# Attention block B of a fused model kernel: projection items, weight fetches and head units in another order, and the compression in one PSUM bank

## Chip, cores and metric

The kernel is one program on one NeuronCore of a Trainium2 chip. The metric is device time in microseconds (us) of one execution, lower is better.

## What is computed

The input is a residual stream x of 256 tokens by 1024 features, all in float32. Four layers of "feed-forward, attention, feed-forward" follow each other; the attention kinds are A, B, C and A again. After them comes one further block, a hybrid of attention and a state-space part (H) with a mixture of experts. The change is about the attention of kind B, layer 1. It has three branches that share the queries; their gated outputs are added:

```python
q, kc, vc, ks, vs, kw, vw, gate = jnp.split(h @ w_in, splits, axis=-1)   # 1024 | 6 x 256 | 48 columns
kc_b = compress_kv(kc, cmp_pos[0], cmp_w1[0], cmp_w2[0])                 # gelu(blocks @ w1) @ w2, 15 blocks
vc_b = compress_kv(vc, cmp_pos[1], cmp_w1[1], cmp_w2[1])
s_cmp = einsum("bsgrd,bngd->bgrsn", q, kc_b) * scale                     # 16 heads x 256 queries x 15
o_cmp = einsum("bgrsn,bngd->bsgrd", masked_softmax(s_cmp), vc_b)
o_slc = selected_block_attention(q, ks, vs, sel_idx, rel_table)          # all 4 blocks chosen: plain causal
o_win = banded_attention(q, kw, vw, rel_table, B_WINDOW)                 # window 512 > 256: plain causal
o = g0 * o_cmp + g1 * o_slc + g2 * o_win
return o.reshape(B, S, -1) @ w_out
```

## The kernel before

Every engine has its own instruction list, written out by hand; semaphores order them. Within an engine the order is fixed: what waits holds up all that stands behind it.

**Weights.** SyncE (SP) streams all weights through a ring of three slots, one "fill" of up to 3 MB after the other, strictly in the order of the list `loads` (`stream_weights`). Fill n may be issued when the last user of fill n-3 is done, and each of its three parts (`sem_raw[0..2]`) when the same part of fill n-1 has landed. Block B has nine fills: `win` (0), the two halves of the query weights `qs[0]`, `qs[1]`, `slc`, `kvc` (the columns of kc and vc), the two first-layer weights of the compression (`b_cmp_w1`, `w1_fill` and the one after it, 2 MB each) and the two halves of `b_w_out`. Before, their order is win, qs[0], qs[1], slc, kvc, w1 of the keys, w1 of the values, w_out, w_out. TensorE waits for all three parts of a fill before its first product with it (`wait_fill`).

**Items.** The input projection is cut into 22 items of 16 matrix products each (`items`; form T gives features on partitions and is evacuated by VectorE, form N gives tokens on partitions and is evacuated by ScalarE). `project(q)` computes item q in a PSUM bank that alternates between 2 and 3. Items 0 to 8 (`ahead`) run before the attention; the others are handed out to the steps by `b["steps"]`. Items with `zc` are the columns that the compression reads, items with `both` are key tiles, each evacuated in four copies.

**Units and steps.** The attention is cut into 24 units: a quad of four heads, a half `a` of the queries (`a` = 0 has 128 keys, `a` = 1 has 256) and a branch `s` (1 window, 0 selected, here called local, 2 compressed, here called short). The first 16 units are scored, the eight short ones are not. Step j of every engine's list holds, in this order on TensorE: scores of unit j, transposes of the probabilities of unit j-2, the items of the step, a part of the compression (`pe_compress`, steps `cmp_step` to `cmp_step` + 4), from step `wo_step` = 22 on an eighth of the output projection (`output_first`), and the value products of unit j-2. VectorE does `coefficients(j-1)`, `biased(j)` (scale, bias, maximum), evacuations, `dve_compress`, `copy_out(j-2)`. ScalarE does `copy_pT(j-2)`, `exps(j)`, evacuations, `act_compress`. GpSimd scales the probabilities (L1715). So a scored unit runs around this loop: scores on TensorE, `biased` on VectorE, `exps` on ScalarE, `coefficients` on VectorE, scaling on GpSimd, transposes on TensorE, copy on ScalarE (L1692), values on TensorE, `copy_out` on VectorE.

Before, the order is the 8 window units, the 8 local units, the 8 short units. Items run in steps 0 to 9 (steps 6, 7 and 8 have two), the compression in steps 10 to 14 with `cmp_blocks` (L1773) made by VectorE in step 9. The two products with `w1` are L1836, the compressed scores are the 64 small products of L1865, and the softmax of the compressed branch is L1792 to L1808. Its probabilities must be there before the first short unit.

After the steps, the second half of the output projection (`output(1, ...)`, L1499) waits in A, B and C for `copy_out` of the last unit:

```python
    pe.wait_ge(K.sem.oT_sb, b["outs"])
    for a in range(NT):
        for half in range(2):
            output(1, a, half).then_inc(K.sem.y_done, 1)
```

Of the kernel before, what the change touches and what calls it, by code (L numbers as in the profile page):

```python
# [17 lines left out]
P = 128  # L18
# [227 lines left out]
class Program:  # L246
# [281 lines left out]
    def mixer_layout(self, b):  # L528
# [19 lines left out]
        if kind == "A":  # L548
# [8 lines left out]
            b["ahead"] = 6  # L557
            b["steps"] = [[6], [7], [8], [9], [10]]
            b["need_qk"] = [4, 6, 8, 10]
            b["need_v"] = [[2, 3]] * 4  # L560
            b["wo_step"] = 6
            wo = ins["a_w_out"][b["j"]]
        elif kind == "B":
            w = ins["b_w_in"][0]
            win = cols(w, (2048, 560))
            qs = [cols(w, (512 * c, 512)) for c in range(2)]
            slc = cols(w, (1536, 512))
            kvc = cols(w, (1024, 512))
            T(win, 0, None, both=4)
# [3 lines left out]
            T(win, 128, None, both=6)  # L573
            for r in range(1, 8):
                Q(qs[r // 4], r)
            T(slc, 0, None, both=0)
            T(slc, 128, None, both=2)
            N(slc, 256, 256, [self.v[:, a, 0:256] for a in range(NT)])
            for kv in range(2):
                for c in range(2):  # L580
                    T(kvc, 256 * kv + 128 * c, None, zc=(kv, c))
# [6 lines left out]
            b["w1_fill"] = len(loads)  # L588
            for kv in range(2):
                loads.append(("rows", ins["b_cmp_w1"][0, kv], 0, CMP_ROW_TILES))  # L590
            wo = ins["b_w_out"][0]
        elif kind == "C":
# [16 lines left out]
            Q(qs[1], 6), K(6), Q(qs[1], 7), K(7), V(1, 1)  # L609
            b["ahead"] = 7  # L610
            b["steps"] = [[7, 8], [9, 10], [11, 12], [13, 14], [15, 16], [17, 18], [19]]
            b["need_qk"] = [5, 9, 13, 18]
# [767 lines left out]
def units_of(b):  # L1380

    att, units, si = b["attn"], [], 0
    if b["kind"] == "H":
        order = [(a, quad, 0) for a in range(NT) for quad in att.quads]
    else:
        order = [(a, quad, s) for s in ((1, 0, 2) if b["kind"] == "B" else (0,)) for quad in att.quads for a in range(NT)]
    for u, (a, quad, s) in enumerate(order):
        scored = s < 2
        units.append(dict(a=a, quad=quad, s=s, si=si if scored else None, q=u, u=u, stage=u // 8, first=True, last=True,
                          nk=N_CMP if not scored else SEQ if b["kind"] == "H" else P * (a + 1)))  # L1390
        si += scored
    return units
# [5 lines left out]

def item_bank(q):

    return 0 if q == 0 else 2 if q % 2 else 3


def pe_mixer(K, pe, b):
# [12 lines left out]
    def product(q, k):  # L1417
        it, bank = items[q], item_bank(q)
# [113 lines left out]
    for j in range(len(units) + 2):  # L1532
        if j < len(units) and units[j]["si"] is not None:
            scores(units[j])
        if j >= 2:
            transposes(units[j - 2])
        for q in b["steps"][j] if j < len(b["steps"]) else ():
            project(q)
        if b["kind"] == "B":
            pe_compress(K, pe, b, j - b["cmp_step"])  # L1540
        if j >= b["wo_step"] and done < 4:
            output_first(done)
            done += 1
        if j >= 2:
            values(units[j - 2])
    while done < 4:
        output_first(done)
        done += 1
    pe.wait_ge(K.sem.oT_sb, b["outs"])
    for a in range(NT):  # L1550
        for half in range(2):
            output(1, a, half).then_inc(K.sem.y_done, 1)


def dve_mixer(K, dve, b):
# [4 lines left out]
    def evacuate_turned(q):  # L1560

        it, bank = items[q], item_bank(q)
        if it["form"] != "T":
# [63 lines left out]
    def copy_out(x):  # L1627
        dve.wait_ge(K.sem.oPV, U0 + x["u"] + 1)
        dst = K.oT[:, 2 * x["quad"]:2 * x["quad"] + 2, x["a"] * P:(x["a"] + 1) * P]
        src = K.psum[:, 6 + x["u"] % 2, 0:2 * P].rearrange("p (t s) -> p t s", t=2)  # L1630
        if x["stage"]:
            dve.wait_ge(K.sem.oT_sb, Q0 + x["u"] - 7)
# [11 lines left out]
    for j in range(len(units) + 2):  # L1644
        if 1 <= j <= len(units) and units[j - 1]["si"] is not None:
            coefficients(units[j - 1])
        if j < len(units) and units[j]["si"] is not None:
            biased(units[j])
        for q in b["steps"][j] if j < len(b["steps"]) else ():
            evacuate_turned(q)  # L1650
        if kind == "B":
            dve_compress(K, dve, b, j - b["cmp_step"])
        if j >= 2:
            copy_out(units[j - 2])


def act_mixer(K, act, b):
# [4 lines left out]
    def evacuate_tokens(q):  # L1662

        it = items[q]
        if it["form"] != "N":
            return
        act.wait_ge(K.sem.proj, b["item0"] + q + 1)
        r2 = K.st[:, PRE_R + it["a"]:PRE_R + it["a"] + 1]
        nc.scalar.activation(it["dst"], K.psum[:, item_bank(q), 0:it["n"]], ACT.Sigmoid if it.get("gate") else ACT.Copy,
                             scale=r2).then_inc(K.sem.evac_act, 1)  # L1670
# [26 lines left out]
    for j in range(len(units) + 2):  # L1697
        if j >= 2:
            copy_pT(units[j - 2])
        if j < len(units) and units[j]["si"] is not None:  # L1700
            exps(units[j])
        for q in b["steps"][j] if j < len(b["steps"]) else ():
# [53 lines left out]
def dve_compress(K, dve, b, step):  # L1756
# [8 lines left out]
    if step == -1:  # L1765
        dve.wait_ge(K.sem.cmp_small, 64)
        wait_evac(K, dve, b, len(b["items"]) - 1)
        for kv in range(2):
# [6 lines left out]
    if step == 2:  # L1775
        dve.wait_ge(K.sem.chidT_ps, 1)
        nc.vector.tensor_copy(K.chidT[:, :, :, :].rearrange("p v j n -> p (v j n)"),
                              K.psum[:, 2, 0:4 * G_B * N_CMP]).then_inc(K.sem.chidT, 1)
    if step == 3:
        dve.wait_ge(K.sem.kcb_ps, 1)  # L1780
        nc.vector.tensor_copy(K.kcb[:, :], K.psum[:, 3, 0:G_B * N_CMP])
        nc.vector.tensor_copy(K.vcb[0:N_CMP, :, :].rearrange("p g d -> p (g d)"), K.psum[0:N_CMP, 2, SEQ:SEQ + G_B * HD])\
            .then_inc(K.sem.kcb, 1)
# [27 lines left out]
def act_compress(K, act, b, step):  # L1811
    nc = K.nc
    if step == 1:
        act.wait_ge(K.sem.slots_used, K.fills[b["fill0"] + b["w1_fill"] + 1][1] + 1)
        nc.scalar.activation(K.chid[0:G_B * N_CMP, :, :],
                             K.psum[0:G_B * N_CMP, 2:4, 0:SEQ], ACT.Gelu_apprx_tanh).then_inc(K.sem.gelu, 1)
    if step == 4:
# [6 lines left out]
def pe_compress(K, pe, b, step):  # L1824
    nc, M = K.nc, G_B * N_CMP
    if step in (0, 1):
# [3 lines left out]
        for j in range(3):  # L1830
            pe.wait_ge(K.sem_raw[j], landed)
        wait_evac(K, pe, b, len(b["items"]) - 1)
        wait_evac(K, pe, b, len(b["items"]) - 2)
        w1 = K.raw[:, slot, 0:CMP_ROW_TILES * SEQ].rearrange("p (r f) -> p r f", f=SEQ)
        for r in range(CMP_ROW_TILES):
            ins = nc.tensor.matmul(K.psum[0:M, 2 + kv, 0:SEQ], K.z2[:, kv, r, :], w1[:, r, :],  # L1836
                                   start=r == 0, stop=r == CMP_ROW_TILES - 1)
        ins.then_inc(K.sem.slots_used, 1)
    if step == 2:
        pe.wait_ge(K.sem.gelu, 1)  # L1840
        for kv in range(2):
            for j in range(2):
                o = (2 * kv + j) * M
                ins = nc.tensor.transpose(K.psum[:, 2, o:o + M], K.chid[0:M, kv, j * P:(j + 1) * P],
                                          K.ident[0:M, 0:M])
        ins.then_inc(K.sem.chidT_ps, 1)
    if step == 3:
# [5 lines left out]
        for g in range(G_B):  # L1853
            for j in range(2):
                ins = nc.tensor.matmul(K.psum[0:N_CMP, 2, SEQ + g * HD:SEQ + (g + 1) * HD],
                                       K.chidT[:, 1, j, g * N_CMP:(g + 1) * N_CMP], K.cw2[:, 1, j, :],
                                       start=j == 0, stop=j == 1)
        ins.then_inc(K.sem.kcb_ps, 1)
    if step == 4:
        pe.wait_ge(K.sem.kcb, 1)  # L1860
        for a in range(NT):
            for h in range(NH):
# [43 lines left out]
def hybrid_bank(q):  # L1906

    return (0, 2, 3, 1, 5)[q] if q < 5 else item_bank(q)

# [1280 lines left out]
```

## Time and profile before

| what | value |
|---|---|
| three timed runs | 2693.93 us median, 2687.63 to 2696.21 |
| the profiled execution | span 2692.0 us from first to last instruction; no separate time of it is given, and the span lies among the three times |
| TensorE busy | 2642.6 us, 98% |
| VectorE, ScalarE, GpSimd busy | 1687.4, 1239.5, 239.1 us |
| mean granted TensorE clock | 0.988 of full speed |
| block B | about 700 to 886 us of the span |

Times in rows are microseconds from the start of the span unless a column says otherwise. A busy TensorE is not a TensorE at its peak: its granted clock is a column of its own.

### The profile page before, as it was taken

The page shows a single profiled execution, that of the slowest core. Times are in us where ns is not written, and L with a number is a line of the kernel's source. Part 1 is how long each engine was busy: PE and PEld are TensorE (multiplying, and loading weights), DVE is VectorE, ACT ScalarE, POOL GpSimd, SP SyncE. Part 2 cuts the span into 40 slices and gives each one's busy share as a digit, 9 for nine tenths or more (in the row PEclk, how much of TensorE's full clock was granted, in tenths as well). Part 3 has the DMA queues.
Part 4 walks back from the last instruction along what each step waited for, and adds up shares of the span by engine and source line. Part 5 has one row for each costly group of instructions (what it writes and reads, how often), then busy time and mean ns, then how long its engine had stood idle before and what let it go on. Part 6 is the DMA issues. An engine that isn't in the chain of part 4 may idle for free.

```text
span 2692.0 us, 36916 instructions
## 1 busy us (share of the span) xinstructions
PE 2642.6 (98%) x13112; PEld 2087.1 (78%) x13112; DVE 1687.4 (63%) x2560; ACT 1239.5 (46%) x1986; POOL 239.1 (9%) x364
## 2 busy tenths in 40 slices
PE   9999999999998999999999999999999999899999
PEld 7887688888874788888768888885888654688887
DVE  6764577777353777775237777745776552577776
ACT  5444544544333545544235455434543222366565
POOL 0001100100111100001010010012000001000000
PEclk9999999999997999999999999999999999999999
DMA  9542455554331555453255546433553322478885
GB/s 322 195 151 88 179 187 187 184 198 159 104 125 62 216 195 191 157 192 136 94 203 196 187 150 221 166 133 144 193 198 114 112 91 73 156 279 287 310 289 196
DMA packets 337244, 472.33 MB, mean 175 GB/s; under 512 B 15632, under 2 KB 275056, under 8 KB 337152
## 3 DMA queue, kind: packets, MB, share of 16 engines
q1 hardware_dynamic: 334464, 464.02, 48.1%
q0 software_dynamic: 2192, 6.94, 0.8%
q8 instruction: 54, 0.88, 0.1%
q14 instruction: 38, 0.31, 0.0%
q10 hardware_dynamic: 496, 0.17, 0.0%
HBM read 470.01 MB, written 1.10 MB: 175 GB/s over the span
## 4 chain that ended last, share of the span: by engine, by line
PE 92%; DVE 4%; ACT 2%; issue 1%; DMA 1%; POOL 0%; SPq 0%; DVEq 0%; ACTq 0%; POOLq 0%
PE psum_all L1298 22%; PE psum_all L1302 12%; PE psum_all L1423 6%; PE psum_all L1350 6%; PE psum_all L1351 6%; PE psum_all L1352 6%; PE psum_all L1499 4%; PE psum_all L1959 4%; PE psum_all L2919 3%; PE psum_all L2900 3%; PE psum_all L2896 3%; PE psum_all L2897 3%; PE psum_all L1426 2%; PE psum_all L2924 1%; PE psum_all L1444 1%; PE psum_all L1463 1%
## 5 line engine op out<-in xcount | busy, mean ns | idle before, releaser
L1298 PE MATMUL psum_all<-hT_both,gu_hi 128*128 128x512 f32 x2688 | 670.9, 391 | 0.3 <-DVE gu_lo L1136 0.3
L1298 PEld LDWEIGHTS psum_all<-hT_both,gu_hi 128*128 128x128 f32 x2688 | 492.8, 188 | 95.4 <-DVE gu_lo L1136 0.6
L1136 DVE TENSOR_TENSOR gu_lo<-raw_ring,gu_hi 128x2048 fp32r<-128x2048 f32 x176 | 402.0, 2286 | 14.1 <-ACT gu_hi L1124 9.6
L1302 PEld LDWEIGHTS psum_all<-hT_both,gu_lo 128*128 128x128 f32 x2688 | 366.7, 190 | 26.2
L1302 PE MATMUL psum_all<-hT_both,gu_lo 128*128 128x256 f32 x2688 | 374.8, 282 | 0.0
L1124 ACT ACTIVATE gu_hi<-raw_ring 128x2048 fp32r (+1 forms) x175 | 334.2, 1912 | 16.1 <-DVE oT L1635 12.2
L1131 ACT ACTIVATE down_hi<-raw_ring 128x1024 fp32r (+1 forms) x240 | 250.6, 1057 | 137.6 <-PE psum_all L1352 108.6
L1143 DVE TENSOR_TENSOR down_lo<-raw_ring,down_hi 128x1024 fp32r<-128x1024 f32 x240 | 292.4, 1218 | 34.1 <-ACT down_hi L1131 34.1
L1350 PE MATMUL psum_all<-down_hi,hidden_hi 128*128 128x512 f32 x704 | 277.2, 394 | 3.3 <-DVE hidden_lo L1230 2.6
L1351 PE MATMUL psum_all<-down_lo,hidden_hi 128*128 128x512 f32 x704 | 276.0, 392 | 0.0
L1352 PE MATMUL psum_all<-down_hi,hidden_lo 128*128 128x512 f32 x704 | 274.0, 389 | 0.0
L1278 POOL TENSOR_TENSOR hidden_hi<-hidden,consts_sb 128x256 fp32r<-128x256 f32 x176 | 108.1, 614 | 1293.4 <-DVE hidden L1226 1274.0
L1164 ACT ACTIVATE silu_gate<-silu_gate 128x256 f32<-128x256 f32 x176 | 73.5, 418 | 237.9 <-DVE silu_gate L1219 237.9
L1423 PE MATMUL psum_all<-hT,raw_ring 128*128 128x256 f32 x800 | 179.8, 380 | 0.0
L2750 DVE TENSOR_TENSOR e_gate_up_lo<-raw_ring,e_gate_up_hi 128x2048 fp32r<-128x2048 f32 x64 | 146.6, 2290 | 32.4 <-ACT e_gate_up_hi L2743 32.0
L1162 ACT ACTIVATE cross_terms<-psum_all 128x256 f32<-128x256 f32 x176 | 67.2, 382 | 214.0 <-PE psum_all L1302 214.0
L1423 PEld LDWEIGHTS psum_all<-hT,raw_ring 128*128 128x128 f32 x800 | 149.2, 190 | 21.1 <-issue 1.8
L1230 DVE TENSOR_TENSOR hidden_lo<-hidden,hidden_hi 128x256 fp32r<-128x256 f32 x176 | 74.8, 425 | 141.3 <-POOL hidden_hi L1278 141.3
L1350 PEld LDWEIGHTS psum_all<-down_hi,hidden_hi 128*128 128x128 f32 x704 | 132.8, 189 | 29.7 <-issue 5.2
L1352 PEld LDWEIGHTS psum_all<-down_hi,hidden_lo 128*128 128x128 f32 x704 | 132.2, 188 | 28.9
L1223 DVE TENSOR_TENSOR up_scaled<-psum_all,cross_terms 128x256 f32<-128x256 f32 x176 | 74.4, 423 | 127.5 <-ACT cross_terms L1166 127.5
L1351 PEld LDWEIGHTS psum_all<-down_lo,hidden_hi 128*128 128x128 f32 x704 | 132.9, 189 | 21.0
(379 smaller groups left out, 3519.4 us busy)
## 6 DMA issues: line engine op xcount, KB each, us to landing
raw_ring<-in_ffn_w_in SPq DMA_DIRECT2D x174, 1024.0 KB, 7.1
raw_ring<-in_w SPq DMA_DIRECT2D x96, 1024.0 KB, 7.8
raw_ring<-in_ffn_w_out SPq DMA_DIRECT2D x88, 1024.0 KB, 9.1
raw_ring<-in_c_w_in SPq DMA_DIRECT2D x12, 768.0 KB, 5.3
raw_ring<-in_w_in SPq DMA_DIRECT2D x10, 768.0 KB, 6.3
gain<-in_norm_g POOLq DMA_DIRECT2D x12, 512.0 KB, 4.0
raw_ring<-in_a_w_in SPq DMA_DIRECT2D x8, 768.0 KB, 5.3
raw_ring<-in_b_w_in SPq DMA_DIRECT2D x8, 768.0 KB, 5.0
```

The source lines that it names most:

```text
L1124: K.nc.scalar.activation(K.gu_hi[:, t, :, :], raw_gu(K, slot, t), ACT.Copy).then_inc(K.sem.gu_hi, 1)
L1131: K.nc.scalar.activation(K.dn_hi[:, t, :], raw_dn(K, slot, t), ACT.Copy).then_inc(K.sem.dn_hi, 1)
L1136: K.nc.vector.tensor_tensor(K.gu_lo[:, t, :, :], raw_gu(K, slot, t), K.gu_hi[:, t, :, :].bitcast(F32), ALU.subtract).then_inc(K.sem.gu_lo, 1)
L1143: K.nc.vector.tensor_tensor(K.dn_lo[:, t, :], raw_dn(K, slot, t), K.dn_hi[:, t, :].bitcast(F32), ALU.subtract).then_inc(K.sem.dn_lo, 1)
L1278: nc.gpsimd.tensor_tensor(K.hid_hi[:, t, :], K.hid[:, t, :], K.one.to_broadcast([P, SEQ]), ALU.mult)\
L1298: nc.tensor.matmul(out, K.gu_hi[:, t, j, :], K.hT_both[:, k, :, :].rearrange("p c s -> p (c s)"), start=k == 0, stop=False)
L1302: return nc.tensor.matmul(out[:, 0:SEQ], K.gu_lo[:, t, j, :], K.hT_hi[:, k, :], start=False, stop=k == KT - 1)
L1350: nc.tensor.matmul(out, h_hi, d_hi, start=first, stop=False)
L1351: nc.tensor.matmul(out, h_hi, d_lo, start=False, stop=False)
L1352: ins = nc.tensor.matmul(out, h_lo, d_hi, start=False, stop=last)
L1423: return nc.tensor.matmul(K.psum[:, bank, 0:SEQ], w[:, k, it["c0"]:it["c0"] + P], K.hT[:, k, :], start=k == 0, stop=k == KT - 1)
L2750: K.nc.vector.tensor_tensor(K.ge_lo[:, t, :, :, :].rearrange("p k g f -> p g k f"), raw_expert(K, b, n, t), K.ge_hi[:, t, :, :, :].rearran ...
```

## The change

Order of the fills in block B: win, qs[0], kvc, qs[1], w1 of the keys, w1 of the values, slc, w_out, w_out. Order of the items from 7 on: Q1 to Q5 (7 to 11), the two key columns of the compression (12, 13), Q6, Q7 (14, 15), its two value columns (16, 17), the first local key tile (18), the local values (19, 20), the second local key tile (21). The steps hold them as 9, 10, 11, 12 and 13, 14, 15, 16 and 17, 18, 19, 20, 21, in steps 0 to 10. The compression runs in steps 8 to 12 (`cmp_blocks` in step 7) and uses bank 3 alone; items after 17 (`zc_last`) use bank 2 alone. The unit order from 8 on is: six local units, two short, one local (`a` = 0, quad 3), two short, the last local, four short. Scores are now taken by scored index, so that the last two local units are still scored in steps 14 and 15, while their transposes come in steps 18 and 21. The last output products wait for the last unit of their own half `a`, in blocks A, B and C.

```diff
-            qs = [cols(w, (512 * c, 512)) for c in range(2)]
+            qs = [cols(w, (0, 512))]
+            kvc = cols(w, (1024, 512))
+            qs.append(cols(w, (512, 512)))
+            b["w1_fill"] = len(loads)
+            for kv in range(2):
+                loads.append(("rows", ins["b_cmp_w1"][0, kv], 0, CMP_ROW_TILES))
             slc = cols(w, (1536, 512))
-            kvc = cols(w, (1024, 512))
...
-            b["steps"] = [[9], [10], [11], [12], [13], [14], [15, 16], [17, 18], [19, 20], [21]]
-            b["need_qk"] = [7, 9, 11, 13, 14, 14, 15, 15]
-            b["need_v"] = [[4, 5]] * 4 + [[16, 17]] * 4
-            b["cmp_step"] = 10
+            b["steps"] = [[9], [10], [11], [12, 13], [14], [15], [16, 17], [18], [19], [20], [21]]
+            b["need_qk"] = [7, 9, 11, 15, 18, 18, 21, 21]
+            b["need_v"] = [[4, 5]] * 4 + [[19, 20]] * 4
+            b["zc_last"] = 17
+            b["cmp_step"] = 8
...
+        local = [(a, quad, 0) for quad in att.quads for a in range(NT)]
+        short = [(a, quad, 2) for quad in (0, 1) for a in range(NT)] + [(a, quad, 2) for a in range(NT) for quad in (2, 3)]
+        order += local[:6] + short[:2] + local[6:7] + short[2:4] + local[7:] + short[4:]
...
+    return 0 if q == 0 else 2 if q % 2 or q > b["zc_last"] else 3
...
-            wait_evac(K, pe, b, q - 2)
+            wait_evac(K, pe, b, q - 1 if q > b["zc_last"] else q - 2)
...
-        if j < len(units) and units[j]["si"] is not None:
-            scores(units[j])
+        if scored_in_step(b, j):
+            scores(scored_in_step(b, j))
...
-    pe.wait_ge(K.sem.oT_sb, b["outs"])
     for a in range(NT):
+        pe.wait_ge(K.sem.oT_sb, Q0 + 1 + max(x["u"] for x in units if x["a"] == a))
...
-            ins = nc.tensor.matmul(K.psum[0:M, 2 + kv, 0:SEQ], K.z2[:, kv, r, :], w1[:, r, :],
+            ins = nc.tensor.matmul(K.psum[0:M, 3, kv * SEQ:(kv + 1) * SEQ], K.z2[:, kv, r, :], w1[:, r, :],
```

## Rows read from the trace of the kernel before

**Rows 1.** Stretches: from:to, length, busy PE, PEld, DVE, ACT, POOL, clock, DMA share, GB/s.

```profile
816.00:851.00 35.00, 24.72 (x154) 13.56 (x153) 16.49 (x49) 11.85 (x34) 4.83 (x3) 0.58 0.03 11
```

**Rows 2.** TensorE by time, steps 6-10: start, length, instruction, [idle before <-releaser].

```profile
761.74 0.65 PE L1486 MATMUL psum_all<-probsT,v_tok 128*64 128x256 f32 x4
...
764.32 3.62 PE L1426 MATMUL psum_all<-raw_ring,hT 128*128 128x256 f32 x16
767.77 3.62 PE L1423 MATMUL psum_all<-hT,raw_ring 128*128 128x256 f32 x16
...
772.34 0.71 PE L1444 MATMUL psum_all<-kT,qT 64*128 64x128 f32 x8
...
790.38 6.90 PE L1836 MATMUL psum_all<-raw_ring,cmp_blocks 128*60 128x256 f32 x31 [1.45 <-DVE cmp_blocks L1773]
```

**Rows 3.** SP in order of time: the issue of one 2 MB fill.

```profile
767.97 1.52 SPq L770 DMA_DIRECT2D raw_ring<-in_b_cmp_w  x3
```

**Rows 4.** DMA of 767 to 777: GB/s in 40 slices; issue to landing.

```profile
GB/s 0 0 0 0 0 0 0 0 139 143 8 12 131 311 389 385 385 385 385 377 389 389 389 389 385 365 373 389 377 389 389 389 389 348 53 0 0 0 0 0
...
raw_ring<-in_b_cmp_w SPq DMA_DIRECT2D x1, 768.0 KB, 7.1
```

**Rows 5.** VectorE in order of time: evacuation of a key tile.

```profile
752.69 1.73 DVE L1576 TENSOR_TENSOR kT<-psum_all,rstd_rows 64x256 f32<-64x256 f32 x4 [1.78 <-PE psum_all L1423]
```

**Rows 6.** TensorE in order of time, step 14 to the end of B.

```profile
816.52 3.75 PE L1865 MATMUL psum_all<-cmp_keysT,qT 64*128 64x15 f32 x64 [0.24 <-DVE cmp_values L1782]
...
820.78 1.54 PE L1444 MATMUL psum_all<-kT,qT 64*128 64x256 f32 x8
...
834.58 1.94 PE L1463 MATMUL psum_all<-consts_sb,scores 128*128 128x128 f32 x8 [2.99 <-POOL scores L1715]
837.63 1.98 PE L1486 MATMUL psum_all<-probsT,v_tok 128*64 128x256 f32 x8 [1.11 <-ACT probsT L1692]
...
847.80 1.03 PE L1457 MATMUL psum_all<-consts_sb,cmp_probs 128*15 128x128 f32 x4
...
850.56 1.03 PE L1457 MATMUL psum_all<-consts_sb,cmp_probs 128*15 128x128 f32 x4
...
871.80 14.00 PE L1499 MATMUL psum_all<-raw_ring,oT 128*128 128x512 f32 x32 [0.53 <-DVE oT L1633]
```

**Rows 7.** Stretches of 2 us around the fall and the rise of the clock.

```profile
820.00:822.00 2.00, 2.00 (x18) 1.14 (x16) 1.86 (x6) 1.22 (x7) 0.72 (x1) 0.85 0.02 4
...
854.00:856.00 2.00, 2.00 (x4) 0.81 (x3) 0.00 (x0) 0.00 (x0) 0.00 (x0) 0.62 0.00 0
```

**Rows 8.** Stretches around a TensorE idle of 2.98 us in the last block.

```profile
2336.00:2340.00 4.00, 1.02 (x6) 0.52 (x4) 2.93 (x19) 2.50 (x5) 0.00 (x0) 1.00 1.10 393
2340.00:2344.00 4.00, 4.00 (x21) 4.00 (x21) 0.00 (x0) 0.98 (x1) 0.00 (x0) 0.54 0.64 262
```

**Rows 9.** The chain that ended last, by time (start, length, what), steps 13 to 16.

```profile
811.47 1.35 ACT scores_first L1677 x7
...
816.47 1.67 ACT scores L1677 x7
...
818.66 0.70 DVE scores_first L1599
...
820.75 0.19 DVE cmp_probs L1792
...
824.32 0.42 DVE oT L1633
...
825.14 1.23 DVE scores L1599
...
827.82 0.32 DVE cmp_probs L1801
...
831.55 0.42 DVE oT L1633
```

**Rows 10.** TensorE at the end of the first A block.

```profile
291.86 8.42 PE L1499 MATMUL psum_all<-raw_ring,oT 128*128 128x512 f32 x19 [0.54 <-DVE oT L1635]
```

More of the change, by code:

```diff
@@ L558, in mixer_layout @@
             b["steps"] = [[6], [7], [8], [9], [10]]
+            b["zc_last"] = len(items)
             b["need_qk"] = [4, 6, 8, 10]
@@ L573, in mixer_layout @@
             T(win, 128, None, both=6)
-            for r in range(1, 8):
+            for r in range(1, 6):
                 Q(qs[r // 4], r)
+            for c in range(2):
+                T(kvc, 128 * c, None, zc=(0, c))
+            for r in range(6, 8):
+                Q(qs[r // 4], r)
+            for c in range(2):
+                T(kvc, 256 + 128 * c, None, zc=(1, c))
             T(slc, 0, None, both=0)
+            N(slc, 256, 256, [self.v[:, a, 0:256] for a in range(NT)])
             T(slc, 128, None, both=2)
[L578 to L581, printed above, removed]
             b["ahead"] = 9
-            b["steps"] = [[9], [10], [11], [12], [13], [14], [15, 16], [17, 18], [19, 20], [21]]
-            b["need_qk"] = [7, 9, 11, 13, 14, 14, 15, 15]
-            b["need_v"] = [[4, 5]] * 4 + [[16, 17]] * 4
-            b["cmp_step"] = 10
+            b["steps"] = [[9], [10], [11], [12, 13], [14], [15], [16, 17], [18], [19], [20], [21]]
[3 more added lines that the diff above has]
+            b["cmp_step"] = 8
             b["wo_step"] = 22
-            b["w1_fill"] = len(loads)
-            for kv in range(2):
-                loads.append(("rows", ins["b_cmp_w1"][0, kv], 0, CMP_ROW_TILES))
             wo = ins["b_w_out"][0]
@@ L610, in mixer_layout @@
             b["ahead"] = 7
+            b["zc_last"] = len(items)
             b["steps"] = [[7, 8], [9, 10], [11, 12], [13, 14], [15, 16], [17, 18], [19]]
@@ L1384, in units_of @@
         order = [(a, quad, 0) for a in range(NT) for quad in att.quads]
-    else:
-        order = [(a, quad, s) for s in ((1, 0, 2) if b["kind"] == "B" else (0,)) for quad in att.quads for a in range(NT)]
+    elif b["kind"] == "B":
+        order = [(a, quad, 1) for quad in att.quads for a in range(NT)]
+        local = [(a, quad, 0) for quad in att.quads for a in range(NT)]
+        short = [(a, quad, 2) for quad in (0, 1) for a in range(NT)] + [(a, quad, 2) for a in range(NT) for quad in (2, 3)]
+        order += local[:6] + short[:2] + local[6:7] + short[2:4] + local[7:] + short[4:]
+    else:
+        order = [(a, quad, 0) for quad in att.quads for a in range(NT)]
+    before = {}
     for u, (a, quad, s) in enumerate(order):
         scored = s < 2
-        units.append(dict(a=a, quad=quad, s=s, si=si if scored else None, q=u, u=u, stage=u // 8, first=True, last=True,
+        units.append(dict(a=a, quad=quad, s=s, si=si if scored else None, q=u, u=u,
+                          stage=(1, 0, 2)[s] if b["kind"] == "B" else 0, adds_to=before.get((a, quad)),
                           nk=N_CMP if not scored else SEQ if b["kind"] == "H" else P * (a + 1)))
+        before[a, quad] = u
         si += scored
@@ L1396, in scored_units, with scored_in_step, item_bank @@
     return [u for u in b["units"] if u["si"] is not None]
-def item_bank(q):
-    return 0 if q == 0 else 2 if q % 2 else 3
+def scored_in_step(b, j):
+    scored = scored_units(b)
+    return scored[j] if 0 <= j < len(scored) else None
+def item_bank(b, q):
+    return 0 if q == 0 else 2 if q % 2 or q > b["zc_last"] else 3
 def pe_mixer(K, pe, b):
@@ L1417, in product @@
     def product(q, k):
-        it, bank = items[q], item_bank(q)
+        it, bank = items[q], item_bank(b, q)
         slot = wait_fill(it["fill"])
@@ L1560, in evacuate_turned @@
     def evacuate_turned(q):
-        it, bank = items[q], item_bank(q)
+        it, bank = items[q], item_bank(b, q)
         if it["form"] != "T":
@@ L1630, in copy_out @@
         src = K.psum[:, 6 + x["u"] % 2, 0:2 * P].rearrange("p (t s) -> p t s", t=2)
-        if x["stage"]:
-            dve.wait_ge(K.sem.oT_sb, Q0 + x["u"] - 7)
+        if x["adds_to"] is not None:
+            dve.wait_ge(K.sem.oT_sb, Q0 + x["adds_to"] + 1)
             ins = nc.vector.tensor_tensor(dst, src, dst, ALU.add)
@@ L1644, in dve_mixer @@
     for j in range(len(units) + 2):
[L1645 to L1648, printed above, removed]
+        if scored_in_step(b, j - 1):
+            coefficients(scored_in_step(b, j - 1))
+        if scored_in_step(b, j):
+            biased(scored_in_step(b, j))
         for q in b["steps"][j] if j < len(b["steps"]) else ():
@@ L1699, in act_mixer @@
             copy_pT(units[j - 2])
-        if j < len(units) and units[j]["si"] is not None:
-            exps(units[j])
+        if scored_in_step(b, j):
+            exps(scored_in_step(b, j))
         for q in b["steps"][j] if j < len(b["steps"]) else ():
@@ L1766, in dve_compress @@
         dve.wait_ge(K.sem.cmp_small, 64)
-        wait_evac(K, dve, b, len(b["items"]) - 1)
+        wait_evac(K, dve, b, b["zc_last"])
         for kv in range(2):
@@ L1777, in dve_compress @@
         nc.vector.tensor_copy(K.chidT[:, :, :, :].rearrange("p v j n -> p (v j n)"),
-                              K.psum[:, 2, 0:4 * G_B * N_CMP]).then_inc(K.sem.chidT, 1)
+                              K.psum[:, 3, 0:4 * G_B * N_CMP]).then_inc(K.sem.chidT, 1)
     if step == 3:
@@ L1815, in act_compress @@
         nc.scalar.activation(K.chid[0:G_B * N_CMP, :, :],
-                             K.psum[0:G_B * N_CMP, 2:4, 0:SEQ], ACT.Gelu_apprx_tanh).then_inc(K.sem.gelu, 1)
+                             K.psum[0:G_B * N_CMP, 3, :].rearrange("p (v f) -> p v f", v=2),
+                             ACT.Gelu_apprx_tanh).then_inc(K.sem.gelu, 1)
     if step == 4:
@@ L1843, in pe_compress @@
                 o = (2 * kv + j) * M
[L1844 removed]
+                ins = nc.tensor.transpose(K.psum[:, 3, o:o + M], K.chid[0:M, kv, j * P:(j + 1) * P],
                                           K.ident[0:M, 0:M])
@@ L1854, in pe_compress @@
             for j in range(2):
-                ins = nc.tensor.matmul(K.psum[0:N_CMP, 2, SEQ + g * HD:SEQ + (g + 1) * HD],
+                ins = nc.tensor.matmul(K.psum[0:N_CMP, 3, SEQ + g * HD:SEQ + (g + 1) * HD],
                                        K.chidT[:, 1, j, g * N_CMP:(g + 1) * N_CMP], K.cw2[:, 1, j, :],
@@ L1860, in pe_compress @@
         pe.wait_ge(K.sem.kcb, 1)
+        wait_evac(K, pe, b, len(b["items"]) - 1)
         for a in range(NT):
@@ L1906, in hybrid_bank @@
 def hybrid_bank(q):
-    return (0, 2, 3, 1, 5)[q] if q < 5 else item_bank(q)
+    return (0, 2, 3, 1, 5)[q] if q < 5 else 2 if q % 2 else 3
 def products_masked(K, n, g):
```

6 lines of the change are left out of this document (2 added, 4 removed).

## Prediction

> **What bounds the kernel now.** I read the busy shares first. TensorE is busy 98% of the span, so time can only be won where it stands still or where its clock is low. Then I went to block B by stretches: from 716 to 816 TensorE is almost always busy at full clock. From 816 to 851 it is busy 24.72 of 35 us at a mean granted clock of 0.58 [rows 1]. TensorE in order of time says why: after the compressed scores there is no item and no compression left to fill the steps, TensorE waits for each unit's softmax, and the eight short units then alternate transposes, copy and values [rows 6]. The clock goes from 1.0 to 0.5, that is from 2.4 to 1.2 GHz, at about 821.3 (the stretch 820 to 822 has 0.85), 4.8 us after the 64 small products L1865 begin; it returns at about 855.5 (0.62 in 854 to 856), some 4 us after the wide output products have begun [rows 7]. Summed from TensorE's waits, B idles about 12 us. Last I looked at the weight queue, because the change reorders the ring, and at the two places outside B that it touches.
>
> **1. The weights of `slc` come too late.** Before, `slc` is fill 3. After, it is fill 6, behind the values' `w1` (fill 5). Fill 5 takes the slot of `kvc` and so waits for item 17, the last that reads `kvc`. SP issues in order, so `slc` cannot start before item 17 is done, although its own slot has been free since item 15. But item 18, the first that reads `slc`, is TensorE's next item, in step 7.
>
> Where is TensorE then? Steps 3 to 6 hold the same items as before except that step 3 has two, and one item costs 3.45 us (from 764.32 to 767.77 in [rows 2]). Item 16 ended at 761.8 and values, scores and transposes took until 764.4, that is 2.6 us [rows 2]. Step 6 has two items, as before, so the second ends at 761.8 + 3.45 = 765.3, and item 18 would start at 765.3 + 2.6 = 767.9.
>
> When does `slc` land? A 2 MB fill was issued at 767.97, immediately after the item it waited for [rows 2, 3]. Its last part, issued about 1.1 us later, landed 7.1 us after its issue: 8.0 us in all, with data moving from about 770 to 775.6, mostly at 385 GB/s [rows 4]. The `slc` fill is the same size and its parts follow those of fill 5 one by one, so I let it continue the stream: 2.1 MB at 385 GB/s are 5.45 us more. It lands at 765.3 + 8.0 + 5.45 = 778.75. TensorE stands 778.75 - 767.9 = **10.8 us**. Bounds: 9.5, if it overlaps better, to 16 - 2.6 = 13.4, if the two fills do not overlap at all. Nothing hides it: item 18 stands before the values and all later steps. The page "DMA: Bandwidth & Descriptors" of the Trainium skill (Anatomy of one DMA) prices a DMA at 2 us plus its bytes at 436 GB/s. By an estimate from it both fills land in 2.0 + 9.6 = 11.6 us instead of my 13.45, and the sum below would be 1.9 us lower; the slices here stay at 385, so I do not use it.
>
> During such a wait the clock falls: after an idle of 2.98 us the stretch 2340 to 2344 has 0.54 [rows 8]. After 4 us of work it is back [rows 7]; about 3.9 us at half clock lose **1.95 us** (0 if the clock held, 3.4 if it came back later). The Trainium skill, "TensorE: Matmul & The Clock Gate" (Loop structure matters more than you think), gives a DMA wait ahead of a matmul as its bad example, after which the matmul runs at half clock. That speaks against this change in just this place; rows 8 agree.
>
> **2. A smaller wait in step 8.** Scores of unit 8 need key tile 18, evacuated in four copies of together 1.73 us [rows 5]. Step 7's values cover 1.02 us, so **0.8 us** remain (0 to 1.5). Item 15, needed in step 6, has one copy of 0.42 us under 1.02 us of values: nothing. Waits on buffers: project(18) waits for item 17's evacuation (1.75 us), under the 2.6 us above; its cost without that cover would be those 1.75.
>
> **3. The waits around the compression go.** `cmp_blocks` is now made beside item 19, so the 1.45 us go [rows 2], with 0.30 for a probability copy behind the Gelu and 0.24 before L1865 [rows 6]: **-2.0 us**. The single bank 3 adds no order that the chain of copies did not already have: Gelu ends during item 21, the copy of the hidden layer 0.8 us before it is needed. The key and value copy stands behind `biased(11)` and is ready about 0.25 us early; if not, it costs under 1 us.
>
> **4. The tail.** Steps 0 to 12 now hold all items and the compression. At the same work, L1865 ends earlier: before, the values of step 14 ended at 820.78 [rows 6]. Without the stall, the same work takes 2.0 less and 0.8 more, 819.55; step 12 after ends before one unit of each size, which took 4.9 us of scores, transposes and values, so at 814.7, and L1865 at 814.1. From there steps 13, 14 and 15 are scored and have no filler. They are bound by one chain through VectorE and ScalarE, because `coefficients(j-1)` stands ahead of `biased(j)`, and `exps(15)` stands ahead of the copy of unit 14. Prices from [rows 9]: compressed softmax part one 3.6 (820.75 to 824.32), copy_out 0.4, coefficients 0.55, biased for 256 keys 2.7 (825.14 to 827.82), part two 3.7 (827.82 to 831.55), copy_out 0.4, coefficients 0.55, biased for 128 keys 2.1 (818.66 to 820.75), exps 1.65 (the 1.35 and the first of the eight), coefficients 0.55, biased 2.7, exps 2.1, then the copy 0.6 and the values of unit 14, 1.1. That is 22.7; with some ten handovers of 0.05 us, 23.3. Unit 14 is finished at 837.4 to 837.6. The clock falls as before, 4.8 us after L1865 starts.
>
> What is then left before the first output product: short units 15, 17 and 18 at 2.76 us each (847.80 to 850.56 [rows 6]), the 128-key unit 16 at 2.85, the 256-key unit 19 at 5.05 (834.58 to 839.6 [rows 6]): 16.2 us, until 853.75. Before, this point was 850.56. From there the rest is the same (35.24 us to 885.80, where the output products of 871.80 end [rows 6]) but for the 0.53 us wait before the last 32 products, which goes. B ends at 853.75 + 35.24 - 0.53 = 888.5 without the stall, **+2.7 us** against 885.8. This contains parts 2 and 3. The interleaving does remove the waits for the last two local units; it pays with three bare scored steps where there was one and five short steps without output products where there were four.
>
> **5. A and C.** The wait of 0.54 before the last output goes in both A blocks [rows 10]; C shows none. **-1.1 us.**
>
> **Sum.** 10.8 + 1.95 + 2.7 - 1.1 = **+14.3 us**. The profiled execution has a span of 2692.0, which becomes 2706.3; it lies 1.9 under the median of the runs, so on the median I predict 2693.93 + 14.3 = **2708.3 us**. Ends: stall 9.5 to 13.4, its clock 0 to 3.4, tail -1 to +5: 2702 to 2714.
>
> **Rivals.** Within 0.3% means 8.1 us, about what a measurement of this kernel can tell from no change.
>
> - *The clock holds through the tail* (not slower). Short steps would take 1.85 us instead of 2.76, unit 19 3.2 instead of 5.05, the first output block 2 us less: 8.6 us less in all, since the chain in part 4 is not TensorE's. +5.7, 2699.6, within 0.3%. It decides from 6.2 us of saved low clock on. For it: L1865 comes after fuller steps. Against: before, the same 64 products came before the same kind of gaps, and the clock never returned while they lasted [rows 1]. 15%.
> - *The fetch is hidden*: `slc` lands before item 18. Needs both fills in 2.6 us; one alone takes 8 [rows 3, 4]. +1.6, 2695.5. 6%.
> - *Both*: -7.0, 2686.9; with a tail better by another microsecond, faster by over 0.3%. 4%.
> - *The stall is longer or hurts more*: fills one after the other and a second fall of the clock in steps 8 to 12, +20, 2714 or above. 12%.
>
> The forecast itself (2703 to 2713) gets 63%. The range 2697 to 2714 leaves out the hidden fetch, the double rival and most of the long stall, about 2 in 10. Slower by over 0.3% (above 2702): 63% + 12% less a little for a cheap stall, 0.73. Within: 0.22. Faster: 0.05.
>
> **What would show it.** One TensorE idle of about 10 to 11 us, put down to the DMA of `b_w_in`, before the first product of step 7, with SP issuing the values' `w1` at about 765.3 and `slc` right behind; clock 0.5 for some 4 us after it. A wait under 1 us before the scores of unit 8. No wait before L1836. Then L1865 ending near 827, unit 14 done near 850, and B ending near 901 instead of 885.8. If B ends before 893, part 1 is wrong; if the stall is there but the low-clock stretch of the tail is short, part 4 is.

## The result and the profile after

| | before | after |
|---|---|---|
| median of 12 runs | 2694.34 us | 2706.4 us |
| profiled execution, span | 2692.0 us | 2707.4 us |
| second scores of B (step 1) to the end of the last 32 output products | 160.6 us | 172.4 us |

The ratio is 1.0047, with a 95% interval of 1.0035 to 1.0059: the change makes the kernel slower, by 12.1 us on the medians (the interval is 9.4 to 15.9 us). One slow execution of 4255.64 us is left out of the ratio; the others lie between 2699.8 and 2709.86, and their median is 2706.24, where that of all twelve is 2706.4. 2708.3 us was predicted.

The length of B in the last row is the one used below to compare traces. It is 885.80 - 725.22 before and 899.41 - 726.99 after. The position of a block's start differs by up to 4 us between profiled executions of these kernels (step 1 begins at 722.9 to 727.0), so the spans alone, 15.4 us apart here, would mislead by a few us.

TensorE of the kernel after, in order of time, steps 7 and 8 (start, length, instruction, idle before it and what ended it); it answers to [rows 2]:

```profile
768.62 1.09 PE L1484 MATMUL psum_all<-consts_sb,scores 128*128 128x128 f32 x8
781.36 5.89 PE L1444 MATMUL psum_all<-hT,raw_ring 128*128 128x256 f32 x16 [11.65 <-DMA raw_ring<-in_b_w_in]
787.18 1.09 PE L1507 MATMUL psum_all<-probsT,v_tok 128*64 128x256 f32 x8
789.07 0.71 PE L1465 MATMUL psum_all<-kT,qT 64*128 64x128 f32 x8 [0.80 <-DVE kT L1597]
```

Item 18 is preceded by one idle of 11.65 us that a DMA of the input weights ends, and its 16 products then take 5.89 us where before 3.62 was usual. The 0.80 us before the scores of unit 8 are there too. The SP queue of the same execution answers to [rows 3]:

```profile
767.07 1.52 SPq L777 DMA_DIRECT2D raw_ring<-in_b_cmp_w  x3
771.46 4.17 SPq L777 DMA_DIRECT2D raw_ring<-in_b_w_in  x3
```

SP issues the values' `w1` at 767.07, when item 17 ends (its products end at 767.04), and the parts of `slc` behind it, each after the same part of `w1` has landed (`x3` are the three parts of a fill). The chain that ended last, by time, shows how that fills the gap:

```profile
768.06 7.17 DMA raw_ring<-in_b_cmp_w
775.25 5.97 DMA raw_ring<-in_b_w_in
781.36 5.90 PE psum_all L1444 x16
```

The last part of `w1` lands at 775.23, only then the last part of `slc` is issued, and it needs 5.97 us more. The data stream behind it has no gap (DMA of 763 to 783, GB/s in 40 slices of 0.5 us; [rows 4] before):

```profile
GB/s 0 0 0 0 0 0 0 0 0 0 88 68 150 377 389 381 385 387 385 361 383 385 391 389 381 397 410 414 397 410 414 410 406 189 29 16 0 0 0 0
```

Busy time in stretches (length, then busy time of PE, PEld, DVE, ACT and POOL, TensorE's clock, DMA share, GB/s), which answers to [rows 1] and [rows 7]:

```profile
773.00:781.00 8.00, 0.00 (x0) 0.00 (x0) 0.00 (x0) 1.58 (x8) 0.00 (x0) 0.50 0.89 339
781.00:785.00 4.00, 3.64 (x9) 2.96 (x10) 0.00 (x0) 0.00 (x0) 0.00 (x0) 0.50 0.00 0
...
790.00:830.00 40.00, 40.00 (x290) 29.38 (x290) 20.28 (x45) 15.05 (x42) 7.76 (x5) 1.00 0.50 178
830.00:834.00 4.00, 4.00 (x20) 2.54 (x17) 3.72 (x12) 2.34 (x10) 0.00 (x0) 0.57 0.16 64
834.00:841.00 7.00, 3.10 (x26) 1.65 (x24) 6.52 (x20) 3.70 (x11) 1.04 (x1) 0.96 0.01 2
841.00:850.00 9.00, 6.50 (x27) 3.96 (x28) 6.37 (x15) 4.03 (x14) 2.94 (x2) 0.50 0.00 0
850.00:854.00 4.00, 2.49 (x17) 0.99 (x16) 1.12 (x5) 1.79 (x6) 1.90 (x1) 0.92 0.00 0
854.00:866.00 12.00, 8.85 (x38) 4.19 (x38) 1.51 (x4) 2.79 (x4) 0.00 (x0) 0.50 0.01 1
```

The clock is at 0.5 (1.2 GHz) during the idle and in the first four us of item 18. From 790 to 830 TensorE has no wait at all. In the tail the clock falls, returns, falls, returns for 4 us and falls again; before, it stayed at 0.5 for 34 us. The tail of TensorE, answering to [rows 6] (the 64 small products, L1865 before, are L1886 here):

```profile
826.13 3.75 PE L1886 MATMUL psum_all<-cmp_keysT,qT 64*128 64x15 f32 x64
...
851.26 0.65 PE L1503 MATMUL psum_all<-probsT,cmp_values 15*64 15x256 f32 x4 [0.83 <-ACT probsT L1710]
...
867.55 3.69 PE L1520 MATMUL psum_all<-raw_ring,oT 128*128 128x512 f32 x8
...
885.41 14.00 PE L1520 MATMUL psum_all<-raw_ring,oT 128*128 128x512 f32 x32
```

Unit 14 (the first short one) ends at 851.9, 25.8 us after the 64 small products begin. The first output product already runs at full clock (3.69), and the last 32 begin without a wait. Before, the first output product took 5.66 us:

```profile
851.38 5.66 PE L1499 MATMUL psum_all<-raw_ring,oT 128*128 128x512 f32 x8
```

### The profile page after: what moved, and what is told of

It reads as the page before. It is cut to its first block, busy times and chain, and to the rows that moved or that the text cites. A ratio compares the mean times of both kernels' runs of the same rounds, so it can differ in the third digit from the quotient of the medians.

```text
span 2707.4 us, 36915 instructions
## 1 busy us (share of the span) xinstructions
PE 2647.4 (98%) x13112; PEld 2092.3 (77%) x13112; DVE 1687.1 (62%) x2560; ACT 1239.6 (46%) x1986; POOL 240.4 (9%) x364
## 4 chain that ended last, share of the span: by engine, by line
PE 91%; DVE 4%; ACT 2%; DMA 1%; issue 1%; SPq 0%; POOL 0%; DVEq 0%; ACTq 0%; POOLq 0%
PE psum_all L1305 22%; PE psum_all L1309 12%; PE psum_all L1444 7%; PE psum_all L1357 6%; PE psum_all L1358 6%; PE psum_all L1359 6%; PE psum_all L1520 4%; PE psum_all L1980 4%; PE psum_all L2921 3%; PE psum_all L2940 3%; PE psum_all L2917 2%; PE psum_all L2918 2%; PE psum_all L1447 2%; PE psum_all L2945 1%; PE psum_all L1465 1%; PE psum_all L1484 1%
```

## The experiments

All times are medians in us, ratios are to the kernel before, measured beside it on the same chip. The runs were made in three batches, e1 to e4, e5 to e8 and e9 to e12, and the kernel before had a median of 2693.47, 2692.74 and 2695.94 in them; so runs of different batches are compared by their ratios and not by their times. "B" is the length defined above, from one profiled execution of each kernel. How far one such length can be trusted is said at e4. Where an expectation counts to the start of the last 32 products, it is 14 us shorter than B.

| run | time | ratio, 95% interval | B |
|---|---|---|---|
| before | 2694.34 | 1 | 160.6 |
| after | 2706.4 | 1.0047 (1.0035 to 1.0059) | 172.4 |
| e1_slc_first | 2690.61 | 0.9991 (0.998 to 1.0003) | 160.0 |
| e2_plain_units | 2695.95 | 1.0016 (1.0004 to 1.0028) | 162.8 |
| e3_half_waits | 2688.41 | 0.9986 (0.9974 to 0.9998) | 159.7 |
| e4_busy_wait | 2704.32 | 1.0045 (1.0028 to 1.0062) | 174.6 |
| e5_cmp10 | 2691.47 | 0.9993 (0.9981 to 1.0005) | 158.5 |
| e6_less_softmax | 2692.58 | 0.9998 (0.9986 to 1.0009) | 158.2 |
| e7_early_output | 2692.38 | 1.0 (0.9989 to 1.001) | 160.8 |
| e8_both | 2691.34 | 0.999 (0.998 to 1.0) | 159.3 |
| e9_filled | 2683.1 | 0.9952 (0.9938 to 0.9965) | 154.0 |
| e10_before_filled | 2684.89 | 0.9957 (0.9943 to 0.9971) | 153.1 |
| e11_cmp10_filled | 2685.47 | 0.9965 (0.9953 to 0.9978) | 152.2 |
| e12_early_filled | 2683.36 | 0.9956 (0.9943 to 0.997) | 154.8 |

### Is it the fetch? (e1_slc_first, e4_busy_wait)

```diff
+            slc = cols(w, (1536, 512))
             b["w1_fill"] = len(loads)
             for kv in range(2):
                 loads.append(("rows", ins["b_cmp_w1"][0, kv], 0, CMP_ROW_TILES))
-            slc = cols(w, (1536, 512))
```

> The changed kernel with one edit: the slc fill stands before the two w1 fills in the list of loads. Theory 1 (the cost is the late fetch of slc): slc is issued when item 9 is done and is long there; the first w1 fill now waits for item 17, lands some 8 us later and is needed only after item 19, so it costs nothing. The 11.65 us idle before item 18 and the slow clock behind it (2.2 us) go: 13.9 us less than the changed kernel, about 2692.5 us, block B from its second scores to the last output product 158.5 us instead of 172.4. Rival (the cost is the new order of steps and units): the idle goes but comes back as a wait for w1 or in the tail, and the time stays above 2700.

The first is the SP queue of e1, then TensorE in order of time:

```profile
763.69 8.49 SPq L777 DMA_DIRECT2D raw_ring<-in_b_cmp_w  x6
```

```profile
766.16 3.62 PE L1444 MATMUL psum_all<-hT,raw_ring 128*128 128x256 f32 x16
769.71 1.09 PE L1507 MATMUL psum_all<-probsT,v_tok 128*64 128x256 f32 x8
771.60 0.72 PE L1465 MATMUL psum_all<-kT,qT 64*128 64x128 f32 x8 [0.80 <-DVE kT L1597]
...
808.67 3.79 PE L1886 MATMUL psum_all<-cmp_keysT,qT 64*128 64x15 f32 x64
...
833.84 0.65 PE L1503 MATMUL psum_all<-probsT,cmp_values 15*64 15x256 f32 x4 [2.15 <-ACT probsT L1710]
```

Item 18 now follows without a wait and at full clock. Both `w1` fills are issued from 763.69 on and neither is waited for. B is 12.4 us shorter than after the change (13.9 expected), the median 15.8; by the ratios it is 15 us. The missing 1.5 us of B are behind the stall: up to the start of the small products the block is 14.1 us shorter (85.06 instead of 99.14), as expected, and from there to its end 1.7 us longer (74.97 instead of 73.28), because the clock lies low at other places. Unit 14 still ends 25.8 us after the small products begin, as in the kernel after. The cause of the loss is the place of `slc` in the list of loads: shown.

```diff
         for q in b["steps"][j] if j < len(b["steps"]) else ():
+            if b["kind"] == "B" and q == 18:
+                keep_clock(K, 24)
             project(q)
```

> The changed kernel with 24 products of no use (128x256, identity times constants, into a free bank; the output is unchanged) put before item 18, so that TensorE works for some 11 us while it would wait. Theory: the wait for slc is by the landing, so item 18 starts no later than before, but at full clock: 3.6 us instead of 5.9, 2.2 us less than the changed kernel, about 2704. Rival: the clock costs nothing, because the next wait (scores of unit 8) takes it back: time unchanged at 2706.4.

TensorE of e4:

```profile
766.69 10.53 PE L1066 MATMUL psum_all<-consts_sb 128*128 128x256 f32 x48
778.85 3.69 PE L1444 MATMUL psum_all<-hT,raw_ring 128*128 128x256 f32 x16 [1.63 <-DMA raw_ring<-in_b_w_in]
...
865.49 5.04 PE L1520 MATMUL psum_all<-raw_ring,oT 128*128 128x512 f32 x8
```

The wait still ends by the landing, and the item takes 3.69 instead of 5.89 us: 2.2 us won at this place, as expected. But B is 2.1 us longer, not shorter. From 850 to 862 this execution has a mean clock of 0.50 where the kernel after has 0.64, and its first output product takes 5.04 us instead of 3.69. The tail gives back more than the item won. The ratio (1.0045 against 1.0047) shows no gain either, but its interval (1.0028 to 1.0062) is too wide to tell the 2.2 us of the theory from nothing.

The kernel after, e1 and e4 have the same steps from the small products on, and this stretch took 73.3, 75.0 and 77.3 us in their profiled executions. The difference lies where the clock is low. So a difference of 1 to 3 us in B between two kernels, each with one trace, is not yet one between their orders of work; this holds for e2, e3 and e5 to e8.

### What is the unit order worth, and the half waits? (e2_plain_units, e3_half_waits)

```diff
-        order += local[:6] + short[:2] + local[6:7] + short[2:4] + local[7:] + short[4:]
+        order += local + short
```

> As the run before, and the units in the old order: 8 window, 8 local, 8 short. Theory 1: steps 12 to 16 hang on the chain through VectorE and ScalarE, which is the same in both orders; the interleaving only lets two short units stand where the last local unit would wait for GpSimd. It is worth about 1 us: B 159 to 160 us, time 2693 to 2694. Rival (the interleaving is what closes the tail): 4 to 6 us slower than the run before.

B is 2.8 us longer than in e1, the median 5.3 us, and the ratio is 0.0025 higher (6.7 us), with intervals that just do not touch (e1 ends at 1.0003, e2 begins at 1.0004). So the theory of 1 us fell, and the interleaving is worth something. How much stays open: the timing is at the rival's 4 to 6 us, the one trace of B is below it. Unit 15 waits for GpSimd again, which the interleaved order does not have (2.99 us in [rows 6]):

```profile
835.92 1.65 PE L1484 MATMUL psum_all<-consts_sb,scores 128*128 128x128 f32 x8 [1.54 <-POOL scores L1736]
```

e3, the kernel before with this part of the change:

```diff
-    pe.wait_ge(K.sem.oT_sb, b["outs"])
     for a in range(NT):
+        pe.wait_ge(K.sem.oT_sb, Q0 + 1 + max(x["u"] for x in units if x["a"] == a))
```

> The kernel before with one part of the change alone: the last output products wait for the last unit of their own half, in A, B and C. Theory: the idle of 0.54, 0.53 and 0.54 us before them goes in A, B and A, C had none: -1.6 us, 2692.7, too little for the timing alone to show. Rival: the end of the block hangs on ScalarE's squares and the next block's weights, and nothing is won: the rows lose the idle, the blocks end no earlier.

B is 0.9 us shorter and the ratio 0.9986. The idle before the last products is gone. The expected 1.6 us lie in the interval (0.9974 to 0.9998, that is a gain of 0.5 to 7 us), which says little of the size.

### What sets the tail? (e5 to e8)

e5, on top of e1:

```diff
-            b["cmp_step"] = 8
+            b["cmp_step"] = 10
```

> The slc-first kernel with the compression two steps later (cmp_step 10, as before the change), all else new. Theory of the chain: with the compression in steps 8 to 12 the steps 13 to 15 have no filler and unit 14 ends 28 to 29 us after L1886 begins; in steps 10 to 14 only step 15 is bare. Worked out from the durations in the trace, unit 14 then ends about 5.6 us earlier and the block from the second scores to the last 32 output products takes 140.5 instead of 146.0 us; time about 2685, ratio 0.997. Rival (early compression is what lets the tail start early): the compressed softmax becomes late for unit 14, the time is the same or worse by a few us.

```profile
817.31 5.02 PE L1886 MATMUL psum_all<-cmp_keysT,qT 64*128 64x15 f32 x64 [0.24 <-DVE cmp_values L1803]
...
833.50 1.01 PE L1478 MATMUL psum_all<-consts_sb,cmp_probs 128*15 128x128 f32 x4 [4.40 <-DVE cmp_probs L1829]
```

Only 1.5 us of 5.5 came. Part of the gain was never there to win: the expectation put the end of unit 14 28 to 29 us behind the start of the small products, and e1 has 25.8. The three bare steps become one, but the compressed softmax is now the last thing that unit 14 waits for (4.40 us), and the clock falls within the small products (5.02 us instead of 3.79). Early compression does buy something, as the rival says.

e6, on top of e1 (the compressed probabilities of the second half of the queries are not normalised):

```diff
             dve.wait_ge(K.sem.cmp_exp, a + 1)
+            if a == 1:
+                nc.vector.tensor_tensor(pc, pc, ok, ALU.mult).then_inc(K.sem.pc, 1)
+                continue
```

> The slc-first kernel, in which VectorE leaves out five of the six operations of part two of the compressed softmax for the second half of the queries (their compressed probabilities are not normalised, so the output is not the reference's). Each takes 0.2 to 0.4 us, 1.45 us together. Theory of the chain: steps 13 to 16 hang on VectorE and ScalarE, so unit 14 ends 1.4 us earlier. Rival (TensorE's clock and its own work set these steps): unit 14 ends at the same distance from L1886.

```profile
811.98 3.75 PE L1889 MATMUL psum_all<-cmp_keysT,qT 64*128 64x15 f32 x64
...
835.53 0.65 PE L1503 MATMUL psum_all<-probsT,cmp_values 15*64 15x256 f32 x4 [2.34 <-ACT probsT L1710]
```

Unit 14 ends 836.18 - 811.98 = 24.2 us after the small products begin instead of 25.8: 1.6 us less for 1.45 us of VectorE work left out. Counted from the end of the small products, which leaves out their own slow clock, it is 22.0 us in the kernel after, 22.0 in e1, 22.5 in e4 and 20.5 here, so this is more than the three others differ. Steps 13 to 16 hang on the VectorE and ScalarE chain. The time of the whole run (0.9998) does not show the gain.

e7, on top of e1, starts the output products two steps earlier (first half of the tokens first); e8 is e7 with `cmp_step` 10:

```diff
-            b["wo_step"] = 22
+            b["wo_step"] = 20
...
+            pe.wait_ge(K.sem.oT_sb, Q0 + 1 + max(x["u"] for x in units if x["a"] == a and x["quad"] < 2))
```

> The slc-first kernel with the first half of the output projection in steps 20 to 23 instead of 22 to 25, the first half of the tokens first, each waiting only for the units that it reads. Theory: of the five bare steps 17 to 21 the last two get fillers, among them the one of 5 us at slow clock, and the clock returns earlier; two bare steps at full clock, 1.85 us each, stand at the end instead. About 3 us less: 143 us from the second scores to the last 32 products, time 2687.5. Rival: only the place of the gaps moves, no change.

> slc first, compression from step 10 and output products from step 20 together. If both theories hold, 5.6 and 3 us add: 137.5 us from the second scores to the last 32 products, about 2682 us, ratio 0.9957 to the kernel before. If they share the same gap (the slow clock of the tail), 141 us and 2686.

```profile
864.00 0.65 PE L1503 MATMUL psum_all<-probsT,cmp_values 15*64 15x256 f32 x4 [0.68 <-ACT probsT L1714]
864.58 0.61 PE L1478 MATMUL psum_all<-consts_sb,cmp_probs 128*15 128x128 f32 x4
865.86 1.11 PE L1503 MATMUL psum_all<-probsT,cmp_values 15*64 15x256 f32 x4 [0.68 <-ACT probsT L1714]
866.91 16.80 PE L1520 MATMUL psum_all<-raw_ring,oT 128*128 128x512 f32 x32
```

The theory of e7 fell: B is 0.8 us longer, not 3 shorter. The two bare steps that moved to the end let the clock fall once more, just ahead of the last products, which take 16.80 us instead of 14.00. e8 has the same (15.7 us) and is 0.7 us shorter than e1, so both of its expectations fell: 159.3 us, where 151.5 was expected if the gains add, and 155 if they share a gap. In e5, e7 and e8 moving gaps about won at most 1.5 us of B, while the clock fell in them.

### Is it the slow clock? (e9 to e12)

The same short product as the kernel's own `keep_clock`, put into the waits, one to nine at a place, into columns of a bank that nobody uses then. In e9, on top of e1 (the tables are given as comments, step: number of products):

```diff
+        if b["kind"] == "B":
+            keep_clock(K, *FILL_STEP.get(j, (0,)))      # before the scores: {15: 4}
         if scored_in_step(b, j):
             scores(scored_in_step(b, j))
...
+        if b["kind"] == "B":
+            keep_clock(K, *FILL_VALUES.get(j, (0,)))    # {13: 2, 14: 5, 15: 2, 16: 5, 17..20: 1, 21: 2}
         if j >= 2:
             values(units[j - 2])
```

> The slc-first kernel with products of no use (128x256, 0.43 us each at full clock, into columns of PSUM that nobody uses) where TensorE waits in steps 13 to 21, as many as fit into the wait; nothing else changed. Theory (the slow clock of the tail is what is left): the clock returns soon after the 64 small products and stays; short steps 1.9 us instead of 2.75, unit 19 3.2 instead of 5.0, first output product 3.6 instead of 5: 6 us less, 154 us instead of 160.0 from the second scores to the end of the last 32 products, time about 2685. Rival: the waits are VectorE's and ScalarE's, the products in them lengthen the steps by what they overshoot: no gain or +1.

> The kernel before with such products in its waits of steps 15 to 21, nothing of the change. If the tail of both kernels loses by the slow clock alone, this one gains as much or more: 152.6 us instead of 160.6, time about 2686. If the interleaved order of the changed kernel is what makes the fillers work, less than 3 us.

> slc first, compression from step 10, and such products in the waits of steps 15 to 21. 152.5 us instead of 158.5 without them, time about 2685.

> slc first, output products from step 20, and such products in the waits of steps 13 to 19, 24 and 25. Without them this kernel's last 32 products ran partly at slow clock (16.8 us instead of 14.0). 153.3 us instead of 160.8, time about 2685. Rival: the last products are slow for another reason and stay at 16.8.

Stretches of e1, the same of e9, then the last products of e9:

```profile
820.00:832.00 12.00, 6.67 (x33) 3.75 (x32) 9.63 (x26) 5.70 (x21) 2.93 (x2) 0.72 0.35 134
832.00:850.00 18.00, 12.33 (x54) 5.68 (x55) 2.77 (x9) 5.17 (x12) 1.89 (x1) 0.61 0.00 1
850.00:862.00 12.00, 12.00 (x39) 5.33 (x38) 1.14 (x3) 1.76 (x3) 0.00 (x0) 0.87 0.00 0
```

```profile
820.00:832.00 12.00, 10.76 (x69) 7.58 (x70) 9.99 (x27) 5.32 (x19) 3.41 (x3) 1.00 0.45 170
832.00:850.00 18.00, 15.68 (x92) 8.78 (x88) 4.92 (x13) 6.51 (x15) 2.01 (x2) 1.00 0.00 1
850.00:862.00 12.00, 12.00 (x46) 5.10 (x45) 1.26 (x3) 1.17 (x2) 0.00 (x0) 1.00 0.01 1
```

```profile
866.03 14.00 PE L1525 MATMUL psum_all<-raw_ring,oT 128*128 128x512 f32 x32
```

The clock is 1.00 from 820 on, where e1 has 0.72, 0.61 and 0.87 in the same three stretches. B is 6.0 us shorter than e1's (6 expected) and the ratio is 0.9952, better than both kernels. The kernel before, with such products in its own waits (e10), gains as much: B 160.6 to 153.1, ratio 0.9957. Its table has eight of them in step 17, between the scores and the transposes, where unit 15 waits for GpSimd. Its stretches:

```profile
820.00:832.00 12.00, 11.24 (x56) 8.23 (x57) 11.10 (x34) 5.84 (x20) 1.37 (x2) 0.86 0.00 1
832.00:850.00 18.00, 16.79 (x90) 9.06 (x89) 2.55 (x6) 4.14 (x7) 1.56 (x1) 1.00 0.00 0
```

e12's last products are back at 14.00 us, so the slow clock had been their cause; e11 has the shortest B, 152.2 (152.5 expected); e12 has 154.8, 1.5 us more than expected. The intervals of the four ratios overlap: no order of steps can be told to be better than another by the time once the clock is held. In B, e10 is 0.9 us shorter than e9, so the new order, without its late fetch, shows no advantage over the old one there.

## Why the prediction was right, point by point

- **Part 1, the late fetch.** 10.8 us predicted, 11.65 measured. `w1` was issued 1.8 us later than I had worked out, as all of B begins 1.8 us later in this execution. The term for the landing was small by 0.7: 14.15 us from the issue of `w1` (767.07 to 781.22) instead of 13.45. The first fill took 8.16 us, not 8.0 (the prediction's own 1.1 and 7.1 are 8.2), and the last part of `slc`, issued only after the last part of `w1` has landed, 5.97 us from there, not 5.45. The clock's share was 1.95 predicted, 5.89 - 3.62 = 2.3 measured; for the upper end of 3.4 that I gave it no row stood. e1 shows that the place in the list is the cause.
- **Part 2.** 0.8 us predicted and 0.80 measured.
- **Part 3.** All three waits are gone; TensorE is busy for 40.00 of the 40 us from 790 to 830.
- **Part 4, the tail.** This term failed in size and in sign. +2.7 us predicted. Measured, the block changed by 11.8 us, of which the stall and its clock are 13.95, so -2.1 in the kernel after; e1, which has no stall, has -0.6. The table splits the block at the start of the small products:

| | second scores to small products | from there to the end |
|---|---|---|
| before | 91.3 | 69.3 |
| predicted, without the stall | 85.1 | 78.1 |
| e1, without the stall | 85.1 | 75.0 |
| after | 99.1 | 73.3 |
| e4 | 97.3 | 77.3 |

  The first column came out. In the second, the chain through VectorE and ScalarE was the right mechanism (e6), and in the kernel after 1.3 us shorter than summed. The other 3.5 us are the rival of the clock in part: it did return in the tail, for seven and for four us, so that some short steps took 1.9 instead of 2.75 us and the first output product 3.69 instead of the 5.66 that it took before. That I had the clock at 0.5 until the output products was the step that was wrong; where the clock stayed lowest, in e4, the tail comes within 1 us of the predicted one. The prediction's own sign against part 4, a short low-clock stretch in the tail, is what the trace shows. The savings that it names for that rival add up to about 7.6 us, not 8.6; about 3.5 came.
- **Part 5.** Both A blocks lose their wait; in the first, the last products start at 291.99, directly behind the values of the last unit. That the blocks end earlier by just 1.1 us was not measured apart from B; e3 as a whole has 0.9986.
- **Sum.** +14.3 predicted, +12.1 measured. By the parts it is 14.3 + 1.2 (part 1 and its clock) - 4.8 (part 4) = 10.7; the last 1.4 us to the timing have no part of their own and lie within its interval. That the total came out so near is in part luck: the two errors had opposite signs. The direction and most of the size are not, since the stall alone is larger than the whole difference.

What stays open: the spans differ by 15.4 us and B by 11.8. 1.8 us of the rest lie before step 1 of B and 1.8 behind it, in code that the change hardly touches. Such differences come and go: behind B the profiled executions took between 1800.8 us (e4) and 1809.2 us (e6), and from 1900 to 2300 us their mean granted clock was 1.00 in e4 and e1 and 0.98 in e6 and in the kernels before and after. Nor did I measure how much of e1's gain over the kernel before is chance; its interval holds 1. And the filled kernels gain more time than their B shows: e9 is 12.8 us under the kernel before beside it (9.4 to 16.7 by the interval), and B, with the 1.1 us expected of the A blocks, gives 7.7.

## What to carry to other kernels

When a list of transfers through a ring is reordered, work out for each fill two times: when its slot comes free *and* when the fills ahead of it in the queue may go. Here a fill whose own slot was free since item 15 stood behind one that waited for item 17, some two and a half us before it was needed. The second thing is the clock. Before, TensorE's waits were short and many in the tail, 10.3 us of the 35 from 816 to 851 [rows 1], and the clock that fell among them cost another 6 to 7.5 us of 160. Products of no use in the gaps won these back, in either order of the work. A change of order in such a stretch should be judged with the clock held, since otherwise a gap that moves changes where the clock is low.

## What I had not expected of the hardware

- In one and the same tail the clock was low at other places from one kernel to the next: with the same steps, the mean clock was 0.66 and 0.50 in two stretches of e4 against 0.69 and 0.64 after, and from the small products to the end of B it took 77.3 us against 73.3 (75.0 in e1).
- Two bare steps of 1.9 us, each with a gap of 0.68 us, and the products around them of 15 rows or columns, were followed by a fall of the clock into wide products that had no gap at all: 16.80 instead of 14.00 us (e7), and 14.00 again with one product of no use in each gap (e12).
